# Relaying, page numbers and the last norm in a hybrid SSM and sparse-attention decoder layer

## The reference, cut to what matters

```
u, q, kv6, gates = columns of rmsnorm(x) @ w_in
branch A: S5 state-space scan of u, gelu, y * sigmoid(y @ w_glu + b_glu)
branch B: sparse attention
    blocks = rows.reshape(nb, 64, kv_head, 64)       # 64 rows are one block
    kcmp   = gelu(flatten(blocks + pe) @ w1) @ w2    # vcmp alike, (64 x 64) -> 64
    rows of a sequence = cache_nsa_kv[page_table]    # 16 pages of 128 rows
                         # [k_cmp, v_cmp, k_sel, v_sel] x 2 heads x 64
x = x + rmsnorm(mixed @ w_out) ; cross-attention ; 
hid = square(relu(rmsnorm(x) @ w_up)) ; x = x + rmsnorm(hid @ w_down) * g_mlp_post
```

## Time and profile before

| | us |
|---|---|
| median of 3 runs | 1343.54 |
| the profiled execution | 1350.1 |
| its span, first to last instruction | 1348.4 |
| PE busy in the span | 1199.8 |
| DVE busy | 631.3 |
| ACT busy | 459.7 |
| POOL busy | 152.2 |

### The profile page before, as it was taken

How to read it: one execution, slowest core, us unless ns; L and a number is a source line. 1 busy time by engine, 2 the same in 40 slices (tenths; PEclk the granted TensorE clock), 3 DMA queues, 4 the chain that set the end, 5 groups by cost and what they waited for, 6 DMA issues and landing times.

```text
span 1348.4 us, 21551 instructions
## 1 busy us (share of the span) xinstructions
PE 1199.8 (89%) x8391; PEld 1055.0 (78%) x8391; DVE 631.3 (47%) x1153; ACT 459.7 (34%) x706; POOL 152.2 (11%) x278
## 2 busy tenths in 40 slices
PE   6999889988997889689997988677999998999994
PEld 5887677666776757478887977577999998999993
DVE  2659667126774550331234643354333334566653
ACT  3100010176665250310003553342323224555542
POOL 0100022251431303100000200010000000000001
PEclk9999879889998889899998999887999998999996
DMA  6742241552643724754128342511332221322101
GB/s 177 182 149 63 90 146 54 113 148 75 166 110 109 241 63 155 221 175 127 61 72 291 125 141 76 177 61 32 95 95 94 75 82 63 110 94 94 63 1 67
DMA packets 155520, 152.86 MB, mean 113 GB/s; under 512 B 41165, under 2 KB 136738, under 8 KB 155210
## 3 DMA queue, kind: packets, MB, share of 16 engines
q1 hardware_dynamic: 146410, 123.82, 30.4%
q0 software_dynamic: 9008, 27.65, 6.6%
HBM read 143.06 MB, written 12.53 MB: 115 GB/s over the span
## 4 chain that ended last, share of the span: by engine, by line
PE 72%; DVE 8%; SPq 7%; issue 4%; ACT 4%; DMA 2%; POOL 0%; DVEq 0%; ACTq 0%; POOLq 0%
PE banks L1332 21%; PE banks L1556 14%; PE banks L893 14%; PE banks L1292 4%; SPq L583 3%; SPq L598 2%; PE banks L1273 2%; PE banks L1077 2%; PE banks L1037 1%; ACT rounded L1748 1%; SPq L615 1%; PE banks L1191 1%; PE banks L1240 1%; PE banks L1112 1%; PE banks L1035 1%
## 5 line engine op out<-in xcount | busy, mean ns | idle before, releaser
L1332 PE MATMUL banks<-rounded 128*128 128x288 f32 (+1 forms) x2304 | 306.3, 295 | 24.1 <-DVE rounded L2615 12.1
L1332 PEld LDWEIGHTS banks<-rounded 128*128 128x128 f32 x2304 | 301.7, 195 | 26.0 <-DVE rounded L2615 13.0
L893 PE MATMUL banks<-arena 128*128 128x272 f32 (+1 forms) x1056 | 253.3, 400 | 7.3 <-DVEq L1994 3.3
L893 PEld LDWEIGHTS banks<-arena 128*128 128x128 f32 (+1 forms) x1056 | 200.3, 192 | 53.1 <-DVEq L1994 3.5
L1556 PE MATMUL banks<-rounded 128*128 128x272 f32 x1536 | 194.9, 290 | 5.9 <-DVE rounded L2750 5.9
L1556 PEld LDWEIGHTS banks<-rounded 128*128 128x128 f32 x1536 | 194.7, 190 | 6.1 <-issue 6.1
L2587 DVE TENSOR_TENSOR rounded<-arena,rounded 128x2048 fp32r<-128x2048 f32 x46 | 105.3, 2291 | 86.7 <-ACT rounded L1748 86.7
L2750 DVE TENSOR_TENSOR rounded<-arena,rounded 128x1088 fp32r<-128x1088 f32 x64 | 82.2, 1291 | 69.5 <-ACT rounded L1952 69.5
L1952 ACT ACTIVATE rounded<-arena 128x1088 fp32r<-128x1088 f32 x64 | 71.2, 1116 | 85.6 <-PE banks L1556 84.5
L1748 ACT ACTIVATE rounded<-arena 128x2048 fp32r<-128x2048 f32 x46 | 87.7, 1908 | 0.0
L855 POOL TENSOR_SCALAR arena<-arena 128x1 f32<-128x1 f32 (+1 forms) x27 | 11.2, 416 | 644.6 <-ACT upper L1731 448.7
(11 more groups left out here) (418 smaller groups left out, 1447.0 us busy)
## 6 DMA issues: line engine op xcount, KB each, us to landing
arena<-in_w_up SPq DMA_DIRECT2D x16, 1024.0 KB, 5.4
arena<-in_w_down SPq DMA_DIRECT2D x16, 1024.0 KB, 5.1
arena<-in_w_in SPq DMA_DIRECT2D x13, 1024.0 KB, 8.4
upper<-in_cache_nsa_kv SPq DMA_DIRECT2D x64, 128.0 KB, 2.8
upper<-in_cache_nsa_kv POOLq DMA_DIRECT2D x64, 128.0 KB, 3.4
arena<-in_w_out SPq DMA_DIRECT2D x8, 1024.0 KB, 5.8
arena<-in_cache_mem_kv SPq DMA_DIRECT2D x16, 512.0 KB, 7.4
arena<-in_cache_nsa_kv SPq DMA_DIRECT2D x90, 64.0 KB, 2.1
```

The lines of the kernel that those rows point to most:

```text
L893: ins = mm(bank(b + h, HALF, rows=M), lhsT(k), rhs[:, k, h * HALF:(h + 1) * HALF], start=(k == 0), stop=(k == K - 1))
L1332: ins = mm(bank(b, N), w[:, k], a[:, k, toks], start=(k == 0 and z == 0), stop=(k == K - 1 and z == 2))
```

## The change

Five things change together.

1. `w1[0]` and `raw_extra` swap homes: the raw extra places are now at R + 9216 (free after `h_ready`), the first half of the compression weights at R + 13312 (free after `y_mm` has reached 8). `KV_AT` changes from (1, 2, 0, 3) to (0, 2, 1, 3). SP and POOL no longer load or clear `w1[0]` ahead of the pages but after tile j = 3 is issued.
2. More page numbers are read ahead: SP reads those of sequence 4 before tile 0 and of 5, 6 and 7 after the tiles 8, 9 and 10; POOL those of 4 and 5 before tile 0 and of 6 and 7 after tiles 8 and 9; `sel_pages` reads all 16 of its chunk before it waits. Tiles 5, 6 and 7 on SP and 6 and 7 on POOL are read page by page as before.
3. Relaying is shared. The first eight relays are on DVE, before `prompt_rows(0)`; of the later 24 half 0 is on DVE (end of the turn) and half 1 on ACT. The copy of the transposed probabilities out of PSUM moves from DVE to ACT, ahead of the exponentials of the turn.
4. The first weight tile but one of the down product is split at step 2 of it and no longer ahead of step 0.
5. The last norm works by channel: DVE copies each bank out times the gain as a per-partition scalar, ACT squares the bank, POOL adds the squares of the first three pairs of channel tiles, PE sums over channels by a product with a column of ones, and after the transposes DVE needs one instruction a tile. Each tile is stored when it is done.

```
-        w1 = [... for at in (9216, 17408)]
+        w1 = [... for at in (13312, 17408)]
-        raw_extra = [place(2048, R + 13312 + x * 2048) for x in range(2)]
+        raw_extra = [place(2048, R + 9216 + x * 2048) for x in range(2)]
-        KV_AT = (1, 2, 0, 3)
+        KV_AT = (0, 2, 1, 3)
...
             if j == 2 or j == 3:
-                eng.wait_ge(sem("y_mm"), 8)
+                eng.wait_ge(*step("h_ready"))
...
+        def relay(eng, copy, j, half):
+            u, k, slot = j // 4, j % 4, raw_slot(j)
+            eng.wait_ge(sem(f"rows_in_{slot}"), 16 + 16 * SP_PAGES * raw_loads(j))
+            eng.wait_ge(sem(f"more_rows_in_{slot}"), 16 * (PAGES - SP_PAGES) * raw_loads(j))
+            if u:
+                eng.wait_ge(sem("cmp_done"), 2 * u - 1 + half)
+            src = raw_rows(j).rearrange("p n (g d) -> p (n g) d", g=2)[:, :, half * 32:half * 32 + 32]
+            signal(copy(relaid[half][:, :, k * 32:k * 32 + 32], src.rearrange("p n d -> p d n")), f"relaid_{half}")
...
         def sel_pages(eng, gg, kc, known):
+            known.update({(gg * 4 + b, p): page for b in range(4)
+                          for (_, p), page in known_pages(eng, (gg * 4 + b,), kc * 4, kc * 4 + 4).items()})
...
-            sp.wait_ge(*step("h_ready"))
-            compress_weights(0, 0)
+            known.update(known_pages(sp, (4,), 0, SP_PAGES))
             for j in range(4 * CU):
...
+                if j in (8, 9, 10):
+                    known.update(known_pages(sp, (j - 3,), 0, SP_PAGES))
...
 (tensor, after the last down step)
+            for t in range(NT):
+                n = tile_rows(t)
+                for j, part in enumerate((ysum, ysq[:, 0], ysq[:, 1])):
+                    ins = mm(bank(0, 1, t, rows=n), part[:, tok0(t):tok0(t) + n], ones, start=(j == 0), stop=(j == 2))
+            signal(ins, "y2_sq")
...
 (scalar, the loop over PAIRS)
-            for i, (qt, r, br) in enumerate(PAIRS):
+            for i in range(NPAIR + 2):
...
+                    signal(fn(pT[:, j % 2, :, 0:n], psum[:, 4:6, 0:n], ACT.Copy), "pT_ready")
...
+                for j in RELAY_AT.get((1, i), ()):
+                    relay(act, lambda o, a: fn(o, a, ACT.Copy), j, 1)
...
 (scalar, end of the up product and the down steps)
-                split_hi(16 + c)
+                if c < 15:
+                    split_hi(16 + c)
...
+                            act.wait_ge(sem("down_out"), 4 * m + 2 * j + h + 1)
+                            signal(fn(ysq[:, j, h * HALF:(h + 1) * HALF], bank(4 * (m % 2) + 2 * j + h, HALF), ACT.Square), "squares")
...
 (vector)
+            for j in range(4):
+                for half in range(2):
+                    relay(dve, cp, j, half)
             prompt_rows(0)
...
+                for j in RELAY_AT.get((0, i), ()):
+                    relay(dve, cp, j, 0)
...
+                        signal(ts(y2T[:, 2 * m + j, h * HALF:(h + 1) * HALF], bank(4 * (m % 2) + 2 * j + h, HALF),
+                                  gpost[:, 2 * m + j:2 * m + j + 1], None, ALU.mult), "down_out")
...
+                signal(stt(x[0:n, t, :], psum[0:n, b0:b0 + 2, :].rearrange("p b c -> p (b c)"), rstd2[0:n, SQ0 + t:SQ0 + t + 1],
+                           x[0:n, t, :], ALU.mult, ALU.add), "y_done")
```

More of the change, by code:

```diff
@@ L359, in hybrid_decoder_layer @@
         h_split = place_r(3 * 4 * TOK, F0).rearrange("p (b z k t) -> p b z k t", b=3, z=2, k=2)
-        gb2 = place(D, F0 + 12 * TOK)
-        xj2 = place(D, F0 + 12 * TOK + D)
+        ysq = place(2 * TOK, F0 + 12 * TOK).rearrange("p (j t) -> p j t", j=2)
+        ysum = place(TOK, F0 + 14 * TOK)
+        ones = sm(1)
         y2T = actT
@@ L474, in hybrid_decoder_layer @@
         squares += [("y1", 4), ("y1", 2), ("x1", 4), ("y1", 3), ("x1", 2), ("x1", 3), ("y1", 0), ("y1", 1), ("x1", 0), ("x1", 1)]
-        squares += [("y2", t) for t in range(NT)]
         square_at = {name: i for i, name in enumerate(squares)}
+        SQ0 = len(squares)
         TILES = (4, 2, 3, 0, 1)
@@ L606, in sel_pages @@
             elif kc == 0:
-                eng.wait_ge(sem("relaid"), relays(13, 1))
+                raw_relaid(eng, 13)
             else:
@@ L786, in _ @@
             signal(pool.memset(x_a[:, 4, :], 0.0), "x_zeroed")
+            signal(pool.memset(ones, 1.0), "ones_set")
             signal(pool.memset(mhalf, -0.5), "mhalf_set")
@@ L840, in _ @@
                     zero_blocks(1, "w1b_zeroed")
+                if j in (8, 9):
+                    known.update(known_pages(pool, (j - 2,), SP_PAGES, PAGES))
             for gg in range(NG2):
@@ L870, in _ @@
             signal(pool.memset(qz, 0.0), "qz_zeroed")
-            inverse_rms(25)
+            inverse_rms(20)
+            for m in range(3):
+                pool.wait_ge(sem("squares"), SQ0 + 4 * m + 4)
+                for j in range(2):
+                    ins = pool.tensor_tensor(ysum, ysq[:, 0] if m == 0 else ysum, ysq[:, j], ALU.add) if m or j else None
+                    if ins is not None:
+                        ins.then_inc(sem("y2_sums"), 1)
+                        pool.wait_ge(sem("y2_sums"), 2 * m + j)
+            pool.wait_ge(*step("y2_var"))
+            for n, c0, c1 in ((P, 0, 4), (TS, 4, 5)):
+                pool.tensor_tensor(rstd2[0:n, SQ0 + c0:SQ0 + c1], var2[0:n, SQ0 + c0:SQ0 + c1],
+                                   mhalf[0:n].to_broadcast([n, c1 - c0]), ALU.pow).then_inc(sem("inverse_rms"), 1)
             pool.wait_ge(sem("mem_stored"), 32)
@@ L1546, in _ @@
                     pe.wait_ge(sem("down_out"), 4 * (m - 1))
+                    pe.wait_ge(sem("squares"), SQ0 + 4 * (m - 1))
                 if t % 4 == 0:
@@ L2328, in prompt_rows @@
                 own.wait()
-                signal(ins, "prompt_rows")
+                signal(ins, ("k_rows", "v_rows")[v])
+            for j in range(4):
+                for half in range(2):
+                    relay(dve, cp, j, half)
             prompt_rows(0)
```

158 lines of the change are left out of this document (76 added, 82 removed).

## The result

The changed kernel takes 1304.72 us (median of 4 runs, 1303.53 to 1309.85) against 1344.49 us for the kernel before beside it; the ratio is 0.9695, 95% interval [0.9667, 0.9723]. The forecast was 1303, range 1291 to 1322. The profiled execution took 1309.85 us with a span of 1308.2, so 40.2 us less span than before, where 40.5 was forecast. The sum is closer than its terms are, and the part on the prediction says why.

The account below looks back on a forecast made before the run. The prediction took PE's stand-stills, behind late gelus, relays and slowly issued pages, as the bound. Its terms a to h summed to 40.5 us, taking the median from 1343.54 to 1303 us, range 1291 to 1322.

Parts of the forecast that it names:

- a: GLU to the loop: shorter PE stop without relays on ACT, less slow clock after; gain 3.7 us, bounds 0 to 5.2.
- b: First gelu of the compression: earlier pages and fewer relays ahead shorten PE's wait; gain 4.7 us, bounds 2 to 5.
- c: Second gelu of the compression: its table load no longer follows a relay; gain 1.3 us, bounds 0 to 1.6.
- d: Third gelu of the compression: early pages of tiles 13 to 15 shrink PE's wait; gain 10.8 us, bounds 8 to 11.
- e: What the loop pays for relays on DVE and copies on ACT: -2.0 us, bounds -6 to 0.
- R1: Rival: the loop becomes bound by DVE, a relay costing 2.0 us like ACT's; 1313 us, chance 0.14.
- f: Samples' second group: numbers read before the wait bring pages earlier, cutting PE's 8.94 us stop; gain 8.5, bounds 5 to 11.5.
- g: Down product: one split less before its start gains 3.0 us (2.9 to 4.7); its steps -0.5 (-5 to 0).
- R4: Rival: POOL and DVE hold each other, at relays against page issues and in the down loop; 1308 us, chance 0.07.
- h: Tail after the last down product: the last norm by channel and earlier stores gain 11 us, bounds 8 to 12.5.
- R2: Rival: pages stay late because ring places come free too late, so early numbers buy little; 1320 us, chance 0.07.
- R5: Rival: more is won, no loop stop lets the clock fall and e costs nothing; 1290 us, chance 0.06.

Follow-up runs that it names:

- the experiment: The changed kernel with only the first eight relays back on ACT, between the GLU units; measured ratio 0.9733 to the kernel before.
- the doubled relay: The changed kernel with each of the 12 relays that DVE does in the loop done twice; measured ratio 0.9715 to the kernel before.
- The faster tail: The changed kernel with DVE adding the two last squares into the sum, so PE has 5 products instead of 15; ratio 0.9696, median 1305.29 us.
- the control: The changed kernel itself, unedited, run once more beside other variants; measured ratio 0.9713 to the kernel before, median 1309.45 us.

## Why the prediction was right, step by step

The direction, the size and the likeliest case were right: late page issue and the relays' place on ACT made the stops. Steps by the prediction's letters:

- **a** was 3.7 and measured 4.2 in this pair, 3.8 by the experiment. The stop fell by 2.4 as worked out (2.2 taken). The clock in the first turn gave 3.1 in this pair and 1.6 by the experiment (1.5 taken). Against that the GLU's 64 matmul records took 17.85 instead of 16.54, but they took 16.6 to 17.9 in kernels with this part and 17.6 and 17.7 in two without it, so that this is not its doing.
- **b, c, d** were stops of 3.5, 1.3 and 9.1 and are 3.45, 0.96 and 9.03. The clock gave back 1.6 behind unit 0 and 1.9 behind unit 2 (1.2 and 1.7 taken). The reason held too: measured from the loop's own start, the 27 transfers end after 12.9 us instead of 20.5, 7.6 earlier (some 9 forecast); without the numbers it is 17.6, with the homes back 16.8. With the numbers read ahead but all relays on ACT, unit 0 stops for 1.09 and unit 2 for 1.08, but unit 1 for 4.28. With the relays moved but no numbers read ahead it is 0.35 and 0.40, and 1.88 and 6.78 follow behind DVE's relay. So early numbers do most for *b* and *d*, the moved relays for *c*. The loop's idle time says why both are needed: 16.3 us before, 8.0 with the numbers alone, 10.5 with the relays alone, 2.4 with both.
- **e** was -2.0. No stop over 0.8 us was added in the loop, so it is 0 to the trace's resolution; the doubled relay shows why. R1 had counted the slack too low, with a turn of 3.9 us: the loop's 32 turns took 139.1 us, 4.3 each.
- **f** was 8.5, 7 of it the stop. Transfers were issued in 26.73 us (26.8 by its working), and PE's idle time in group 1 fell by 7.0: the stop of 8.94 went whole, and the 2.2 us for the window cache came. The clock, counted at +1.5, took 0.6: L1222's first 32 records, ahead of the first chunk's scores, took 6.55 instead of 3.69 us, and what was slow behind the old stop was 2.6 quicker. Group 1 is 6.3 us shorter (29.81 to 23.48), inside [5, 11.5].
- **g** was 3.0, measured 3.0, and 0.9 of stops in the steps (0.5 taken). The stops go with the old tail (0.0) and not with the old split (0.9): R4's mechanism, POOL's adds against DVE, at a fifth of its price (last section).
- **h** is the mis-sized term: 11 taken, 8.5 measured, inside [8, 12.5]; the tail of 19.28 us is just above the 16 to 19 that the prediction gave as its sign. The 32 records of the earlier trace rows were read as 32 products, and they are 16 (4 x 4 in the loops at L1118), so that a product costs 0.234 and not 0.117. At half clock the 15 then take 5.66, 0.38 each. The faster tail bears it out: 5 products, 10 records, 1.90 us.
- **What had no term:** 5.3 us lost ahead of the GLU, 5.5 won between the loop and group 1, 3.4 between group 1 and down. Nearly all of it is PE at another clock. The terms themselves come to some 36.4 of the 40.5 us forecast (*f* and *h* 2.2 and 2.5 short), and these stretches add 3.6. The sum's error of 0.3 us is therefore luck; another profiled execution of this same kernel is 6.4 us longer.

R1 and R3 fell by the 1.05 us relay. R2 fell too: the changed kernel without part 2, at 0.9814 of 1343.54 = 1318.5, has about the time that R2 was priced at (1320), and the changed kernel is 15 us away from it. R4's two places were both found (last section), and only the one in the down loop reached PE. R5 was right that *e* costs nothing, but its 1290 did not come, with *f* and *h* short and slow clock left in the loop (granted 0.50 at 339.5 to 341.4).

## What to carry to other kernels

Where an engine waits for a transfer ahead of work that others need, giving that instruction to another engine only moves the wait to that queue; the transfer has to be early as well. Before judging a few us from two profiles, compare the idle time of the bounding engine stage by stage: for the same code it was 108.3 and 109.8 us, where the busy time moved from 1199.9 to 1204.8. Count instructions by the program and records by the trace before dividing a row's time by its count.

## What the runs showed of the hardware

**DVE and POOL hold each other.** The Trainium skill, "SBUF — State Buffer", section "SBUF: two separate sides", has an exclusive lock between them, which no row of before showed; now rows do. Two kinds of instructions meet in the changed kernel's down loop: a POOL add, which takes 1.36 us where only one is due, and DVE's split of a weight tile, which takes 2.29 us elsewhere.

```profile
1193.38 3.74 POOL L895 TENSOR_TENSOR upper<-upper 128x544 f32<-128x544 f32 x2 [46.92 <-ACT upper L1996]
...
1196.07 3.20 DVE L2616 TENSOR_TENSOR rounded<-arena,rounded 128x2048 fp32r<-128x2048 f32 x1 [0.18 <-ACT rounded L1780]
```

Two adds took 3.74 instead of 2.7, and the split that began beside the second took 0.9 us more. This happens twice, and PE stops for 0.45 us each time. Under the GLU, DVE's relays run back to back, and a POOL memset of 64 x 2048 stretches to three times its time:

```profile
274.22 5.79 POOL L845 MEMSET upper<- 64x2048 f32 x1 [1.41 <-PE banks L1085]
```

With the relays on ACT both memsets of this line take 1.80. One relay beside a memset took 2.62 us instead of 1.05. The rule of the Trainium skill, that the loser waits for the whole of the other's instruction, fits that relay. For the memset it is too little: DVE's eight relays and four small copies follow on each other to 278.27, and the memset ends 1.74 us after them, about its own length. In all five profiles in which it starts under them it ends 1.73 to 1.75 us after the last copy. So it seems to run only when DVE's whole unbroken run is over. In the profiles in which it starts later, POOL's two stores ahead of it are held instead, here in the control, where DVE's run ends at 278.07:

```profile
270.71 7.48 POOL L507 DMA_DIRECT2D out<-arena  x2
```

With the relays on ACT these two take 1.07. None of this reached PE there: the stop before the loop is 1.71 or 1.72 us in every profile with the relays on DVE. What length of gap on DVE lets POOL in was not tried.

**A stop costs clock behind it.** 7.7 us of standing still cost about 2.4 us more, 2.0 of it in the first three groups of matmuls after it; the granted clock was 0.62 in the mean of the 13 us around it (399 to 412 us), where the changed kernel without the stop had 1.00 from 399.5 to 419.5.
